# A two-model kernel on one Trainium2 core: three pieces of work are moved one unit of the weight stream later

## The chip, the cores and the metric

The kernel is one program on one core of one Trainium2 chip. The metric is the device time of one execution in microseconds, the median of several runs. Lower is better.

## What is computed

Two small models stand one behind the other, batch 1, 256 tokens, width 1024, all in float32. The first has two layers. Layer 0 mixes by gated linear attention, layer 1 by a recurrent mixer (mLSTM), and behind each mixer stands a mixture of 16 experts in which each token uses two:

```python
def mlstm_mixer(x, ...):                       # the recurrent mixer, 4 heads of 256
    qk, v, o_pre, gates = split(x @ w_in)
    q, k = split(silu(causal_conv(qk)))
    ... s = einsum('bhid,bhjd->bhij', q_n, k_n) * p
    num = ... + einsum('bhij,bhje->bhie', s, v_n);  den = ... + s.sum(-1)
    h = num / maximum(abs(den), exp(-m_row))
    return (head_norm(h) * sigmoid(o_pre)) @ w_out
def grouped_moe(t, ...):
    for e in range(16):
        h = silu(t @ w1[e]) * (t @ w3[e]);  y = y + gates[:, e:e + 1] * (h @ w2[e])
```

The second model has two layers of attention (8 query heads of one kind, 12 dilated ones in three groups) with rotary positions, a gate, and a feed-forward block of width 4096:

```python
    qa = axial_rope(rms(qa, q_norm_a[l]), row_cs, col_cs)      # rotation over rows and columns
    qb = apply_rope(rms(qb, q_norm_b[l, g]), *seq_cs)          # rotation over the sequence
```

## The kernel before, in words

**Weights and engines.** 420 MB of weights stream from HBM in chunks of 1 MB (128 x 2048 floats). SP issues every load in one fixed order and waits, chunk by chunk, until the buffer's last readers are done (`load`). A chunk is two *units* of 128 x 1024. Outside the experts a unit is split in two: ACT writes its rounded part `hi` (L1661), DVE the rest `lo` (L2111), and PE multiplies in three products. There are five `hi` and five `lo` buffers, so ACT may write unit n only when PE has used unit n-5. Experts' units are read unsplit.

**Order of the work.** There is one fixed list of steps per stage, written by a generator (`walk_gla`, `walk_moe`, `walk_mlstm`, `walk_attention`, `walk_ff`). Each engine runs through the same list and picks out its own part of each step, so moving a step moves it on PE, ACT and DVE alike. Waits are semaphores between the engines. Within an engine nothing overtakes.

**Side work.** `run_a` and `run_b` yield the matmuls of one projection, a job per unit, and behind each job call a function that advances a list of side steps (`Side.advance(n)` takes the next n of them). In the recurrent mixer the last projection before the output one is `og` (output gate, 8 jobs, numbered 0 to 7 here). Beside it run: the last head's scores (PE, then their weighting on DVE, L2104 `AR<-ps,AR`), four `values` steps on PE (each a few 128x1 products for the denominator, then 128x256 products), `den` (denominator, DVE from L2660), two `norm_stats` (L2275) and `norm_scale` (L2282 to the second L2104), `norm` 0 and 1 (ACT, L1705, four instructions each), `gated` 0 (DVE, L2104 `AR<-AR`, two instructions). An iterator `pace` says how many side steps follow each `og` job. Ahead of job 7 `gate_first` runs what is left, and PE turns (transposes) the gated rows, L991 (`turn` 0 and 1).

**Experts.** `walk_moe` first sorts tokens to experts. `gather` (g, k) is eight PE matmuls of 256 columns that collect rows for expert group g, columns 256k to 256k+255. Its result is written by ACT for even k in group 0 (L1821) and by DVE for odd k (L2101). Then come jobs `up` of 8 matmuls, four units each. The first one (job 0 here) reads gathers 0 and 1, the second (job 1) gathers 2 and 3.

**Attention.** The `qkv` projection has six segments of four jobs each. Behind a segment follow its rotation steps on DVE: sum, inverse root, norm, one `rope_turn` per rotation (segments 1 and 3 in `SEGS` have two, the others one) and `rope_add` (L2823). Then `qk_turn` on PE (L1491) turns its rows, and ACT copies them (L1987). `turns` holds how many jobs are still to pass before that, at first `LAG` = 2.

The longer of the two `pace` lists is:

```python
    pace = iter((0, 1, 2) + 13 * (3,))
    yield from run_b("og", 2, 8, feed, lambda: side.advance(next(pace)), end=gate_first)
```

Of the kernel before, what the change touches and what calls it, by code (L numbers as in the profile page):

```python
# [158 lines left out]
def run_a(name, mt, kt, feed, tick=None):  # L159
    for what, n, i in walk_a(mt, kt):  # L160
        if what == "unit":
            u, split = feed.unit()
            yield from split
        elif what == "mm":
            yield (name, n, i, u)
        elif what == "sink":
            yield (name + "_out", n)
        elif tick:
            yield from tick()
# [133 lines left out]
def walk_moe(feed, key):  # L303

    yield ("constants",)
    for g in range(4):
        yield ("ln_turn", g)
    yield ("router",)
    yield ("ln_stats",)
    yield ("logits",)  # L310
    yield ("sum_up", key)
    yield ("fill", 1)
    yield ("rows", 0, 0)
    yield ("affinity",)
    yield ("rows", 1, 0)
    yield ("x_hi", 0)
    for t in range(2):
        yield ("rows", t, 1)
    yield ("x_hi", 1)
    yield ("sum_row", key)  # L320
    yield ("ranks",)
    yield ("count",)
    yield ("x_lo", 0, 0)
    yield ("fill", 0)
    yield ("places",)
    yield ("one_hot", 0)
    yield ("x_lo", 1, 0)
    for t in range(2):
        yield ("x_lo", t, 1)
    for k in range(3):  # L330
        yield ("gather", 0, k)

    def beside(p, s):

        if s == 0:
            if p == 0:
                yield ("gather", 0, 3)
                yield ("sum_turn", key)
                for t in range(2):
                    yield ("ln_x", t, 0)  # L340
                    yield ("ln_x", t, 1)
                yield ("gates",)
                yield ("sum_out", key)
            if p in (0, 2, 4):
                yield ("one_hot", p // 2 + 1)
            if p == 1:
                yield ("turn", 0)
        if p > 1:
            for n in range(2):
                if s == (1 if p < 8 else 4):  # L350
                    yield ("scatter", p - 2, n)
        if p < 8 and s == (1 if p else 3):
            yield ("maps", p)
        if p == 7 and s == 1:
            yield ("overflow",)
        if p == 2 and s == 2:
            for n in range(2):
                yield ("carry", n)
        if 0 < p < 8 and s == 4:
            yield ("turn", p)  # L360
        if p < 6:
            for k, at in enumerate((1, 4) if p else (2, 3)):
                if s == at:
                    yield ("gather", p // 2 + 1, 2 * (p % 2) + k)

    for p in range(9):
        for s in range(6):
            if (p == 8 and s < 4) or (p == 0 and s > 3):
                continue
            us = []  # L370
            for _ in range(4):
                u, split = feed.unit()
                us.append(u)
                yield from split
            if s < 4:
                yield ("up", p, s // 2, s % 2, tuple(us))
            else:
                yield ("down", p - 1, s - 4, tuple(us))
            if s in (1, 3):
                yield (("silu", "gated")[s // 2], p)  # L380
            elif s > 3:
                yield ("y", p - 1, s - 4)
            yield from beside(p, s)
    for n in range(2):
        yield ("scatter", 7, n)
    yield ("open",)
    yield ("z_stats",)


def walk_mlstm(feed):  # L390
    def gates():
        yield []
        yield [("g_rows",)]
        yield [("g_cols",)]
        yield [("log_f", 0)]
        yield [("log_f", 1)]
        yield []
        yield [("f_cum",)]
        yield [("f_turn",)]
        yield [("run_max", 0)]  # L400
        yield [("run_max", 1)]
        yield [("run_max", 2)]
        yield []
        yield [("max_cols",), ("p_logits", 0)]
        yield [("p_logits", 1)]
        yield [("p_exp",)]
        yield [("p_mask",)]

    done = set()

    def scores():
        for h in range(4):
            while 2 * h + 1 not in done:
                yield []
            yield []
            yield [("scores", h)]

    def values():
        for hp in range(2):
            for t in range(2):  # L420
                yield [("values", t, hp)]
        yield [("den",)]
        yield [("norm_stats", 0)]
        yield [("norm_stats", 1)]
        yield [("norm_scale",)]
        yield [("norm", 0)]
        yield [("norm", 1), ("gated", 0)]

    side = Side(gates())
    yield from run_b("v", 2, 8, feed, side.advance)  # L430
    side.parts.append(scores())
    later = []
    for job in run_a("qk", 16, 8, feed, side.advance):
        if job[0] == "qk_out":
            done.add(job[1])
        if job[0] == "lo" and 6 in done:

            later.append(job)
            continue
        yield job  # L440
    yield from later
    side.parts.append(values())

    def gate_first():
        yield from side.drain()
        yield ("ln_gains",)
        yield ("turn", 0)
        yield ("turn", 1)

    pace = iter((0, 1, 2) + 13 * (3,))  # L450
    yield from run_b("og", 2, 8, feed, lambda: side.advance(next(pace)), end=gate_first)
    route = routing()
    rows = iter([[("ln_x", t, s)] for t in range(2) for s in range(2)] + 4 * [[]])
    yield from run_b("o", 2, 8, feed, lambda: route() + next(rows), half=lambda: (("turn", 2), ("turn", 3)), halved=True, staggered=True)


SEGS = [([(0, 8, 0)], []), ([(0, 2, 1), (128, 4, 2)], [(384, 2, 0)]), ([(0, 4, 3)], [(256, 4, 128)]),
        ([(0, 4, 4), (256, 4, 5)], []), ([(0, 4, 7)], [(256, 4, 384)]), ([(0, 4, 6)], [(256, 4, 640)])]
# [27 lines left out]
LAG, D1, D2 = 2, 3, 4  # L486
# [24 lines left out]
def walk_attention(feed, sums):  # L511
    turns, pending, pairs = [], [], []

    def rope(n):
        yield [("rope_sum", n)]
        yield [("rope_inv", n)]
        yield [("rope_norm", n)]
        for q in range(len(SEGS[n][0])):
            yield [("rope_turn", n, q)]
        turns.append([LAG, n])  # L520
        pending.append(n)
        yield [("rope_add", n)]

    def due():
        for x in list(turns):
            x[0] -= 1
            if x[0] < 0:
                turns.remove(x)
                pending.remove(x[1])
                yield ("qk_turn", x[1])  # L530

    def attention():
        while pending:
            yield []
        for j in range(PAIRS + D2):
            if j < PAIRS:
                due = [x for x in EXP_AT if EXP_AT[x] == j]
                yield [("score", j)] + [("exp", x) for x in due]
            if 0 <= j - D1 < PAIRS:
                yield [("probs", j - D1)]  # L540
            if j - D2 >= 0:
                i, n, of, *_ = SETS[2 * (j - D2)]
                if n == of - 1:
                    pairs.append(i)
                yield [("value", j - D2)]

    def with_turns(name, jobs):

        for job in jobs:
            if job[0] == name:  # L550
                yield from due()
            yield job

    side = Side()
    yield ("tables",)
    for job in with_turns("qkv", run_b("qkv", 6, 8, feed, lambda: side.advance(2))):
        yield job
        if job[0] == "qkv_out" and job[2] == 1:
            side.parts.append(rope(job[1]))
    side.parts.append(attention())  # L560
    yield from with_turns("gate", run_a("gate", 16, 8, feed, lambda: side.advance(2)))
    while len(pairs) < 2:
        yield from side.advance()
    yield from run_a("bb", 8, 2, feed, lambda: side.advance(2))
    yield from side.drain()
    side.parts.append(spread(0))
    yield from side.advance()
    yield from run_a("ba", 8, 4, feed, side.advance)
    yield from side.drain()
    yield from run_b("o", 2, 8, feed, halved=True, staggered=True, after=sums_up(sums))  # L570
# [2701 lines left out]
```

## Time and profile before

| | |
|---|---|
| Median of 3 runs | 1484.76 us (1483.83 to 1485.95) |
| Profiled execution, its own time | 1485.66 us |
| Profiled execution, span of the instructions | 1483.8 us |
| PE busy | 1443.6 us |
| DVE, ACT, POOL busy | 910.2, 626.7, 40.8 us |
| DMA | 420.17 MB, mean 283 GB/s |

The profiled execution's own time is 1.9 us longer than its span. Start and end of the program lie in that difference. Where the stages lie in the span: gated linear attention to 118 us, its experts to 332, recurrent mixer to 490, its experts to 711, then attention and feed-forward twice. A timeline row merges neighbouring instructions of one kind. In it the bracket gives the idle time of the engine just before and what ended it. A float32 product can leave two records on PE, so a count there can be twice the number of instructions.

### The profile page before, as it was taken

The numbers are of one execution on the slowest core, as the hardware profiler recorded it, in microseconds if no ns is written. First come the engines' busy times: TensorE is split into PE (matmuls) and PEld (weight loads), VectorE is DVE, ScalarE is ACT, GpSimd is POOL, SyncE is SP. The second block draws the span as 40 slices with busy tenths as digits, with TensorE's granted clock in tenths as the row PEclk, the third lists the DMA queues.
The fourth block names the chain that finished last, engine by engine and source line by source line (L and its number), as shares of the span: only waits on it lengthen the run. The fifth ranks groups of instructions, "written<-read, shape, count | busy, mean of one in ns | idle before, by whom it ended". The sixth has DMA issues, their size and how long they took to land.

```text
span 1483.8 us, 20474 instructions
## 1 busy us (share of the span) xinstructions
PE 1443.6 (97%) x8383; PEld 1068.5 (72%) x8383; DVE 910.2 (61%) x1549; ACT 626.7 (42%) x1004; POOL 40.8 (3%) x39
## 2 busy tenths in 40 slices
PE   9999999989999999999799999999999999999998
PEld 7885444436888544443578897999988898799997
DVE  4986111118787611111799888997968976775555
ACT  6453211115334321211555655454456566465443
POOL 0000000000000000000210000000002000000000
PEclk9999999999999999999899999999999999999999
DMA  9897999998467899999665463899955533445540
GB/s 379 314 365 301 426 427 426 427 426 329 166 247 297 331 424 427 427 426 426 247 231 184 181 232 142 335 369 352 357 182 187 197 123 125 151 170 193 179 168 29
DMA packets 59062, 420.17 MB, mean 283 GB/s; under 512 B 6657, under 2 KB 6721, under 8 KB 8658
## 3 DMA queue, kind: packets, MB, share of 16 engines
q1 hardware_dynamic: 58322, 417.17, 71.5%
q0 software_dynamic: 640, 1.61, 0.4%
q8 instruction: 69, 1.13, 0.3%
q14 instruction: 31, 0.25, 0.0%
HBM read 417.71 MB, written 1.05 MB: 282 GB/s over the span
## 4 chain that ended last, share of the span: by engine, by line
PE 80%; DVE 11%; DMA 4%; ACT 3%; issue 1%; SPq 0%; DVEq 0%; ACTq 0%
PE ps L869 78%; DVE lo L2111 2%; DMA AR<-in_moe 2%; DMA raw<-in_moe 2%; DVE AR L2104 2%; PE ps L1520 1%; DMA AR<-in_wgu 1%; DVE AR L2101 1%; PE ps L1491 1%; ACT AR L2011 1%; PE ps L1244 1%; DVE TINY L2104 1%; DVE ACC L2104 0%; PE ps L991 0%; PE ps L1001 0%
## 5 line engine op out<-in xcount | busy, mean ns | idle before, releaser
L2111 DVE TENSOR_TENSOR lo<-raw,hi 128x1024 fp32r<-128x1024 f32 x296 | 359.4, 1237 | 97.7 <-ACT hi L1661 97.0
L1661 ACT ACTIVATE hi<-raw 128x1024 fp32r<-128x1024 f32 x296 | 306.2, 1056 | 183.3 <-PE ps L869 178.1
L869 PE MATMUL ps<-T,hi 128*128 128x256 f32 x1792 | 323.8, 283 | 1.4 <-DVE lo L2111 0.6
L869 PE MATMUL ps<-hi,T 128*128 128x512 f32 x896 | 285.8, 396 | 1.0 <-DVE lo L2111 0.6
L869 PEld LDWEIGHTS ps<-T,hi 128*128 128x128 f32 x1792 | 277.1, 189 | 10.0 <-issue 5.1
L869 PE MATMUL ps<-T,lo 128*128 128x256 f32 x896 | 249.2, 280 | 0.0
L869 PEld LDWEIGHTS ps<-hi,T 128*128 128x128 f32 x896 | 169.0, 189 | 38.0 <-DVE lo L2111 2.1
L869 PE MATMUL ps<-lo,T 128*128 128x512 f32 x448 | 172.8, 390 | 0.0
L869 PEld LDWEIGHTS ps<-T,lo 128*128 128x128 f32 x896 | 169.2, 189 | 0.3 <-DVE lo L2111 0.3
L869 PE MATMUL ps<-hi,AF 128*128 128x512 f32 x512 | 163.3, 391 | 0.0
L2104 DVE SCALAR_TENSOR_TENSOR AR<-AR,ps 128x512 f32<-128x512 f32 x52 | 35.4, 684 | 192.0 <-PE ps L869 104.8
L869 PE MATMUL ps<-raw,TF 128*64 128x512 f32 x424 | 128.2, 595 | 3.0 <-issue 3.0
L869 PE MATMUL ps<-AR 128*64 128x512 f32 (+7 forms) x612 | 108.6, 408 | 4.7 <-POOL AR L2907 1.3
L869 PEld LDWEIGHTS ps<-hi,AF 128*128 128x128 f32 x512 | 96.2, 188 | 19.5
L869 PE MATMUL ps<-AR,TF 128*64 128x512 f32 x328 | 107.7, 595 | 0.5 <-DMA AR<-in_moe 0.5
L1857 ACT ACTIVATE AF<-ps,TINY 128x512 fp32r<-128x512 f32 x32 | 22.0, 688 | 195.5 <-PE ps L869 195.5
L2104 DVE SCALAR_TENSOR_TENSOR AF<-ps,TINY,AF 128x512 fp32r<-128x512 f32 x32 | 24.0, 750 | 124.6 <-ACT AF L1857 124.6
L869 PE MATMUL ps<-lo,AF 128*128 128x512 f32 x256 | 99.9, 390 | 0.0
L869 PEld LDWEIGHTS ps<-lo,T 128*128 128x128 f32 x448 | 84.5, 189 | 16.8
L869 PEld LDWEIGHTS ps<-raw,TF 128*64 128x64 f32 x424 | 39.5, 137 | 63.2 <-issue 62.4
L869 PEld LDWEIGHTS ps<-AR 128*64 128x64 f32 (+2 forms) x612 | 58.8, 163 | 33.6 <-issue 20.8
L2104 DVE SCALAR_TENSOR_TENSOR ACC<-raw,TINY,ACC 128x2048 f32<-128x2048 f32 x28 | 65.6, 2344 | 0.2
(247 smaller groups left out, 1730.5 us busy)
## 6 DMA issues: line engine op xcount, KB each, us to landing
raw<-in_moe SPq DMA_DIRECT2D x76, 1024.0 KB, 17.1
raw<-in_b_ff SPq DMA_DIRECT2D x64, 1024.0 KB, 5.3
AR<-in_moe SPq DMA_DIRECT2D x59, 1024.0 KB, 17.1
raw<-in_ada SPq DMA_DIRECT2D x48, 1024.0 KB, 6.7
ring<-in_moe SPq DMA_DIRECT2D x45, 1024.0 KB, 15.8
raw<-in_b_in SPq DMA_DIRECT2D x24, 1024.0 KB, 6.0
raw<-in_b_gate SPq DMA_DIRECT2D x16, 1024.0 KB, 4.8
ACC<-in_moe SPq DMA_DIRECT2D x12, 1024.0 KB, 20.2
```

The costliest lines, as they stand in the source:

```text
L869: return e.matmul(o, l, r, start=a, stop=z, skip_group_check=True)
L1244: ins = e.transpose(p[:, 128 * f:128 * f + 128], m.GR[:, 128 * f:128 * f + 128], ident)
L1491: ins = e.transpose(p[:, 256 * x + 128 * q:256 * x + 128 * q + 128], m.RT[n % 2][:, q, 128 * (p0 + x):128 * (p0 + x) + 128], ident)
L1520: ins = e.transpose(p[:, 256 * k + 128 * q:256 * k + 128 * q + 128], m.PB[j % 8][:, q, 128 * k:128 * k + 128], ident)
L1661: e.activation(hi[n % NC][:, :], raw[place[c]][:, 1024 * half:1024 * half + 1024], ACT.Copy).then_inc(*to("hi", "hi", n))
L1857: e.activation(m.YH[:, HALF[n]], PS[bank["down", i, x, n]][:, :], ACT.Copy, scale=m.GS[:, x:x + 1]).then_inc(*to("tile_out", "y_hi", i, x, n))
L2011: ins = e.activation(o, src, ACT.Exp, scale=m.SC, bias=mx[:, q:q + 1], accum_out=sm[:, 2 + 2 * k + q:3 + 2 * k + q])
L2101: return e.tensor_scalar(o, a, s1, s2, op0=op0, op1=op1)
L2104: return e.scalar_tensor_tensor(out=o, in0=a, scalar=s, in1=b, op0=op0, op1=op1)
L2111: tt(lo[n % NC][:, :], r, hi[n % NC][:, :], SUB).then_inc(*to("lo", "lo", n))
```

## The change

Three edits in the step lists, with no work added or removed.

1. Experts: `gather` (0, 2) is put behind job 0, next to `gather` (0, 3).
2. Recurrent mixer: `pace` is 0, 0, 1, 3, 3, ... in place of 0, 1, 2, 3, 3, ...
3. Attention: the turn of a segment with two rotations comes one job later (`LAG` + 1). The other segments stay.

```diff
@@ walk_moe
-    for k in range(3):
+    for k in range(2):
         yield ("gather", 0, k)
     def beside(p, s):
         if s == 0:
             if p == 0:
-                yield ("gather", 0, 3)
+                for k in (2, 3):
+                    yield ("gather", 0, k)
                 yield ("sum_turn", key)
@@ walk_mlstm
-    pace = iter((0, 1, 2) + 13 * (3,))
+    pace = iter((0, 0, 1) + 13 * (3,))
@@ walk_attention, rope(n)
-        turns.append([LAG, n])
+        turns.append([LAG + len(SEGS[n][0]) - 1, n])
```

Lines behind L337 have a number one higher in the changed kernel. POOL and SP keep their order in every row.

**DVE, recurrent mixer, from the last `conv` step to the denominator.** `AR<-ps,AR 128x384` weights the last head's scores, `ACC<-raw,TINY,ACC` is a step of the second model's modulation, the copy at the end opens `den`. Before:

```order
L2104 SCALAR_TENSOR_TENSOR AR<-AR 128x512
L2111 TENSOR_TENSOR lo<-raw,hi 128x1024 x3
L2104 SCALAR_TENSOR_TENSOR AR<-ps,AR 128x384
L2104 SCALAR_TENSOR_TENSOR ACC<-raw,TINY,ACC 128x2048
L2111 TENSOR_TENSOR lo<-raw,hi 128x1024 x2
L2660 COPY TINY<-ps 128x8
```

Now:

```order
L2105 SCALAR_TENSOR_TENSOR AR<-AR 128x512
L2112 TENSOR_TENSOR lo<-raw,hi 128x1024 x3
L2105 SCALAR_TENSOR_TENSOR ACC<-raw,TINY,ACC 128x2048
L2112 TENSOR_TENSOR lo<-raw,hi 128x1024
L2105 SCALAR_TENSOR_TENSOR AR<-ps,AR 128x384
L2112 TENSOR_TENSOR lo<-raw,hi 128x1024 x2
L2661 COPY TINY<-ps 128x8
```

The weighting now stands behind the modulation step and one more `lo`, and a further `lo` comes ahead of the denominator.

**ACT, recurrent mixer, around the norm.** `AR<-ps,TINY` are the eight norm instructions (four for each half of the heads), `T<-ps,TINY` follows the turn. Before:

```order
L1925 ACTIVATE AR<-ps 128x512 x2
L1661 ACTIVATE hi<-raw 128x1024 x2
L1705 ACTIVATE AR<-ps,TINY 128x256 x8
L1661 ACTIVATE hi<-raw 128x1024
L1714 ACTIVATE T<-ps,TINY 128x256 x4
```

Now:

```order
L1926 ACTIVATE AR<-ps 128x512 x2
L1662 ACTIVATE hi<-raw 128x1024 x2
L1706 ACTIVATE AR<-ps,TINY 128x256 x4
L1662 ACTIVATE hi<-raw 128x1024
L1706 ACTIVATE AR<-ps,TINY 128x256 x4
L1715 ACTIVATE T<-ps,TINY 128x256 x4
```

A `hi` part now stands between the two halves of the norm. On DVE its `lo` part stands ahead of the two `gated` instructions, behind which it stood before:

```order
L2296 TENSOR_TENSOR TINY<-TINY 128x8
L2105 SCALAR_TENSOR_TENSOR TINY<-TINY 128x8
L2112 TENSOR_TENSOR lo<-raw,hi 128x1024
L2105 SCALAR_TENSOR_TENSOR AR<-AR 128x512 x2
L2105 SCALAR_TENSOR_TENSOR T<-ps,TINY,T 128x256 x4
L2112 TENSOR_TENSOR lo<-raw,hi 128x1024
```

This is the changed order. Before, one `lo` stood behind `AR<-AR 128x512 x2` as well as the one ahead of it, and the `lo` ahead of it was of the unit before, which now stands between the two tokens' halves of `norm_stats`.

## Rows read from the trace of the kernel before

**Rows 1.** Page, part 1: busy us (share of the span) and instructions.
```profile
PE 1443.6 (97%) x8383; PEld 1068.5 (72%) x8383; DVE 910.2 (61%) x1549; ACT 626.7 (42%) x1004; POOL 40.8 (3%) x39
```

**Rows 2.** Timeline of PE, mixer's end: start, us, line, operation, count [idle before <-releaser].
```profile
440.69 1.55 PE L869 MATMUL ps<-AR 128*128 128x256 f32 x8 [1.29 <-DVE AR L2104]
442.00 0.47 PE L869 MATMUL ps<-hi,T 128*128 128x512 f32 x1
...
452.85 0.95 PE L869 MATMUL ps<-cst,AR 128*128 128x1 f32 x8
...
455.29 0.58 PE L869 MATMUL ps<-hi,T 128*128 128x512 f32 x1
...
463.46 0.39 PE L869 MATMUL ps<-hi,T 128*128 128x512 f32 x1
464.42 1.06 PE L991 MATMUL ps<-cst,AR 128*128 128x128 f32 x8 [0.57 <-DVE AR L2104]
...
468.51 0.47 PE L869 MATMUL ps<-hi,T 128*128 128x512 f32 x1 [0.25 <-DVE T L2104]
```

**Rows 3.** Timeline of DVE, the same stretch.
```profile
443.87 0.55 DVE L2104 SCALAR_TENSOR_TENSOR AR<-ps,AR 128x384 f32<-128x384 f32 x1
444.34 2.34 DVE L2104 SCALAR_TENSOR_TENSOR ACC<-raw,TINY,ACC 128x2048 f32<-128x2048 f32 x1
...
453.84 0.17 DVE L2660 COPY TINY<-ps 128x8 f32<-128x8 f32 x1 [4.89 <-PE ps L869]
...
461.41 0.17 DVE L2104 SCALAR_TENSOR_TENSOR TINY<-TINY 128x8 f32<-128x8 f32 x1
...
463.58 0.69 DVE L2104 SCALAR_TENSOR_TENSOR AR<-AR 128x512 f32<-128x512 f32 x1 [0.22 <-ACT AR L1705]
466.35 1.23 DVE L2111 TENSOR_TENSOR lo<-raw,hi 128x1024 fp32r<-128x1024 f32 x1 [2.08 <-ACT hi L1661]
```

**Rows 4.** Timeline of ACT, the same stretch.
```profile
461.61 3.76 ACT L1705 ACTIVATE AR<-ps,TINY 128x256 f32<-128x256 f32 x8 [2.10 <-DVE TINY L2104]
465.22 1.10 ACT L1661 ACTIVATE hi<-raw 128x1024 fp32r<-128x1024 f32 x1
```

**Rows 5.** Timeline of PE, start of attention layer 0.
```profile
756.89 1.97 PE L1491 MATMUL ps<-cst,AR 128*128 128x128 f32 x8 [2.65 <-DVE AR L2823]
```

**Rows 6.** Windows of 1 us: PE, PEld, DVE, ACT, POOL busy, PEclk, DMA share, GB/s.
```profile
729.00:730.00 1.00, 1.00 (x6) 0.87 (x5) 1.00 (x3) 0.91 (x2) 0.00 (x0) 0.95 0.00 0
759.00:760.00 1.00, 1.00 (x4) 0.77 (x3) 0.97 (x2) 0.49 (x1) 0.00 (x0) 0.59 0.64 156
```

**Rows 7.** Timeline of PE, ahead of attention, after its longest wait.
```profile
719.76 4.63 PE L869 MATMUL ps<-XLO 128*128 128x512 f32 x10 [6.65 <-DVE X L2104]
```

**Rows 8.** Timeline of ACT, then DVE, start of the first experts.
```profile
129.07 1.02 ACT L1821 ACTIVATE TF<-ps,vec 128x256 f32<-128x256 f32 x2 [1.18 <-PE ps L869]
...
130.01 1.00 DVE L2101 TENSOR_SCALAR TF<-ps,vec 128x256 f32<-128x256 f32 x2 [0.68 <-PE ps L869]
...
140.22 1.23 DVE L2207 TENSOR_TENSOR X<-X,AR 128x1024 f32<-128x1024 f32 x1
```

**Rows 9.** Timeline of SP's DMA issues, both experts' starts.
```profile
141.47 0.33 SPq L3005 DMA_DIRECT2D AR<-in_moe  x1
...
513.50 0.80 SPq L3005 DMA_DIRECT2D raw<-in_moe  x2
```

**Rows 10.** Windows of 4 us, both experts' starts, columns as in rows 6.
```profile
144.00:148.00 4.00, 4.00 (x24) 1.76 (x22) 0.24 (x1) 1.02 (x2) 0.00 (x0) 1.00 1.01 422
508.00:512.00 4.00, 4.00 (x24) 2.19 (x24) 2.48 (x4) 0.00 (x0) 0.00 (x0) 1.00 0.81 272
```

**Rows 11.** Waits of PE: line <- releaser: us in total, times, longest.
```profile
PE ps L1491 <- DVE AR L2823: 3.7, 2, 2.6
```

**Rows 12.** Timeline of PE, then DVE, second segment of attention layer 1.
```profile
1148.20 0.82 PE L1491 MATMUL ps<-cst,AR 128*128 128x128 f32 x6
...
1146.73 0.96 DVE L2823 TENSOR_TENSOR AR<-AR 128x768 f32<-128x768 f32 x1
```

## Prediction

> **What bounds the kernel now.** I read the page's busy times first: PE works 97% of the span [rows 1]. PE's work is the same before and after, so the edits can only change how long PE stands still. I then read the timelines of PE, DVE and ACT side by side at the places where steps move, looking for the bracket that shows a wait, and for the experts SP's issues and the DMA windows, since there the weights can be the bound.
>
> Three things are to be seen. In the recurrent mixer PE waits 1.29 us ahead of the last head's scores, 0.57 us ahead of the turn and 0.25 us ahead of the output projection [rows 2]. In the experts' stage the DMA engines are full from shortly after its start (share 1.01, 422 GB/s) [rows 10], so the stage ends when the stream ends, and the stream's last gap decides. In attention PE waits for a rotation twice in the whole program, 3.7 us together [rows 11].
>
> **Recurrent mixer, the scores.** The last scores follow `og` job 1 before and job 2 now. The 1.29 us wait goes: PE has job 2 (2.85 us) to run first. One job is (463.85 - 455.29) / 3 = 2.85 us, 463.85 being 463.46 + 0.39 [rows 2]. Without the wait job 1 ends at 440.69 - 1.29 = 439.40, job 2 at 442.25, the scores (442.00 - 440.69 = 1.31) at 443.56, job 3 at 446.41. Now the `values` steps stand there, and they need the weighted scores. DVE's weighting has moved behind the modulation step and one `lo`. DVE is free for the modulation step at 443.87 [rows 3]. That takes 2.3 and a `lo` 1.15 (rows 2.34 and 1.23, less the overlap with what follows of nearly 0.1), the weighting 0.55: ready at 447.87. PE starts 0.15 behind it, as at the turn (463.58 + 0.69 against 464.42), so at 448.0: **1.6 us of new wait**. Its bounds are 0, if DVE runs through faster than these rows, and 1.9. This is the first wait that takes the place of the one removed.
>
> **Recurrent mixer, the denominator.** Before, the last `values` step is behind job 3, and its denominator products end at 452.85 + 0.95 = 453.80 [rows 2]. DVE's copy starts at 453.84, after 4.89 us of standing idle [rows 3], so PE sets it. Now three `values` steps follow job 3 and the fourth job 4. The same point comes at 453.80 - 1.29 + 1.6 + 2.85 = 456.96, or 3.15 us later.
>
> **Recurrent mixer, from there to the turn.** DVE's chain of copy, statistics and scale has one `lo` in its middle before and now, and takes 453.84 to 461.58 [rows 3]. Before, ACT starts the norm at 461.61 (3.76 us for eight, so 1.88 for the first four), and the second `gated` instruction starts at 463.58. PE turns at 464.42, which is 2.84 us behind the scale [rows 2 to 4]. Now a `hi` stands between the norm's halves and its `lo` ahead of `gated`. Behind the scale come the four norms 1.9, `hi` until DVE starts its `lo` 1.13 (465.22 to 466.35), `lo` 1.15, two `gated` 1.3 (2 x 0.69 less the overlap), and 0.15 until PE starts: 5.63 us, **2.8 us longer**. The `hi` itself isn't late: it needs job 5, over by then. So the turn starts 3.15 + 2.8 = 5.95 us later, at 470.4. PE would get there at 463.85 - 1.29 + 1.6 = 464.2 and stands for 6.2 us where it stood for 0.57. The output projection's 0.25 us wait goes, as the turned rows then have job 7 as cover without DVE's `lo` in front.
>
> **TensorE's clock.** After a wait of 2.65 us PE starts again at 756.89 with the same kind of work, eight transposes and then 12-matmul jobs [rows 5], and the granted clock is at its lower level (1.2 GHz) until about 759.82 (mean 0.59 in that microsecond) [rows 6]. That is 2.9 us at half speed, a loss of 1.5. After the 6.65 us wait at 719.76, with a gap in the restart, the higher level returns only at about 729.1 [rows 6, 7]. For 6.2 us I take a loss of **1.5 us**, the nearer row in the work that follows. The ends are 0 and 4.0 (half of some 8 us of work in the second row). The Trainium skill, "TensorE: Matmul & The Clock Gate", section "Why this matters for your kernels", warns against exactly such gaps between bursts of matmuls, and its Part 1 says that one kernel had 6, 11 or 14 slow matmuls from run to run. At its 427 against 216 ns for 512 columns that is an estimate of 1.3 to 3.0 us, by which the sum would be up to 1.5 us higher.
>
> The mixer's part is 5.95 + 1.5 - 0.25 = **+7.2 us**. What waits for it further on moves with it: SP frees the experts' buffers in the mixer by the scores, the values, the gated rows and the norm, and behind them by PE's jobs.
>
> **Does the DMA stream swallow it?** In the second experts' stage the windows show a gap at the start (0.81 in 508 to 512) [rows 10]. SP can only issue the next loads once job 1 is done, 513.50 [rows 9]. A late PE makes this point late, and no load is ahead of it, so the delay passes 1:1.
>
> **Experts' third gather.** One gather is 0.94 us (ACT starts on gather 0 at 129.07, DVE on gather 1 at 130.01). Job 0 now follows gather 1 at once, but needs ACT's copy of gather 0, done at 129.07 + 1.02 = 130.09 [rows 8]. PE would come at 129.95 and starts at 130.15, **+0.2 us**. Job 0 frees two chunks some 0.7 us earlier, which is worth nothing if a later event rules the stream. In the first stage that event is the end of the normed rows X on DVE (140.22 + 1.23, SP issues at 141.47) [rows 8, 9], started by gather 3, which is 0.2 later. In the second it is job 1. So each stage costs 0.2, both **+0.4 us**. The bounds are -0.7 and +0.4 for each.
>
> **Attention's turns.** Of the twelve turns four move. The moved ones didn't wait: at 1148.20 there is no bracket, the sum was ready at 1147.69 [rows 12]. The two waits in the program are on the first segment's turn, with one rotation, which isn't moved. Nothing is to be gained and the transposes just stand between other jobs. Their readers (ACT's copy, the rotation two segments later, the scores) come later. I take 0, between 0 and +0.4 (0.1 for each).
>
> **Sum.** 7.2 + 0.4 + 0 = +7.6 us. On the profiled execution's own 1485.66 us this gives 1493.3. That execution is 0.9 above the median, and on the median the forecast is 1484.76 + 7.6 = **1492.4 us**. With the clock's loss at 0 or 4.0, the scores' wait at 0 or 1.9 and the gathers at their bounds, the case runs from 1487.7 to 1496, though all ends on one side are unlikely.
>
> **Rivals.**
> - *The mixer gains, as its 1.29 us wait goes and nothing is late.* The place is the turn ahead of job 7. It decides if `gated` is done before PE arrives at about 464. Then 1.29 + 0.57 + 0.25 go and 0.4 comes: 1483.1, no slower than before. For it speaks that DVE idles 4.89 us ahead of the copy; against it, that it idles because PE's products are late, which the change makes later. 7%. If the closed DMA gaps also count 0.7 each, it is near 1481.3; that needs both, 4% beside it.
> - *The stream swallows the delay.* If loads were queued beyond the slip when the second experts start, PE would catch up while it waits for weights: about 1485.2. The gap in 508 to 512 speaks against it. 6%.
> - *The clock returns late*, as after 719.76: 4.0 lost in place of 1.5, 1494.9. 12%, inside the range.
> - *Only the denominator's delay counts* (the new `hi` and `lo` cost nothing): 7.6 - 2.8 = 4.8, 1489.6. It decides if ACT starts that `hi` before the norm, which its order forbids. 8%, inside too.
>
> **How the numbers follow.** The forecast has 63%; with the last two rivals 83% lie at 1487.7 or more, so slower by over 0.2%. The range reaches from 1487.0, so that a partly swallowed delay is in it, to 1495.5. About 0.2% (3 us) is what a measurement of this kernel can tell from no change. Slower by more: 83%. Within it: 12%, the first and the second rival less one per cent. Faster by more: 5%, that one and the 4% beside the first rival.
>
> **What would show it.** In the changed profile PE should wait about 1.5 us ahead of the first 128x1 products, for DVE `AR` L2105, and about 6 us ahead of L992, followed by some 3 us of granted clock 0.5. The 1.29 us ahead of the scores should be gone, DVE's copy L2661 should start 3 us later, and ACT's norm should be split by a `hi`. The first job of each experts' stage should wait 0.2 us for ACT's `TF`. The attention rows should keep their distances. The forecast is wrong if PE's wait ahead of L992 is under 2 us, or if the second experts' stage ends less late than it begins.

## The result, and the profile after

The changed kernel takes **1497.62 us** (median of 4 runs, 1495.62 to 1499.07), against 1485.36 us (4 runs, 1483.83 to 1486.03) of the kernel before. The ratio is 1.0083, 95% interval 1.0066 to 1.0101: slower by 12.3 us, where 7.6 had been forecast. The sign and the places were right; the time lies 5.2 us above the forecast and 2.1 us above the range. Of the 5.2 us, 0.6 is that the kernel before has a median of 1485.36 with its fourth run and had 1484.76 with three.

The page of the changed kernel, parts 1 and 2 (busy time, then the span in 40 slices), answers to [rows 1]:

```profile
span 1496.3 us, 20472 instructions
...
PE 1447.8 (97%) x8383; PEld 1072.3 (72%) x8383; DVE 913.1 (61%) x1549; ACT 626.4 (42%) x1004; POOL 39.3 (3%) x39
...
PEclk9999999999998999999899999999999999999999
```

The number of PE's instructions is unchanged, yet PE is busy 4.2 us longer than the 1443.6 of before: the same work took more time. The slice of 449 to 486 us shows a clock of 8 tenths. (Lines of helpers behind L337 are one higher in the changed kernel, so L869 reads L870.) The timeline of PE in the mixer's end shows where that is (start us, us, line, operation, count [idle before <-releaser]); compare [rows 2]:

```profile
442.37 1.47 PE L870 MATMUL ps<-AR 128*128 128x256 f32 x8
...
446.22 0.39 PE L870 MATMUL ps<-hi,T 128*128 128x512 f32 x1
448.39 0.59 PE L870 MATMUL ps<-cst,AR 128*128 128x1 f32 x4 [1.78 <-DVE AR L2105]
448.84 2.06 PE L870 MATMUL ps<-AR 128*128 128x256 f32 x4
450.69 1.71 PE L870 MATMUL ps<-cst,AR 128*128 128x1 f32 x8
452.25 3.64 PE L870 MATMUL ps<-AR 128*128 128x256 f32 x8
...
456.09 1.11 PE L870 MATMUL ps<-AR 128*128 128x256 f32 x4
...
459.79 0.95 PE L870 MATMUL ps<-cst,AR 128*128 128x1 f32 x8
460.59 1.97 PE L870 MATMUL ps<-AR 128*128 128x256 f32 x8
...
474.03 1.94 PE L992 MATMUL ps<-cst,AR 128*128 128x128 f32 x8 [6.01 <-DVE AR L2105]
```

Two things are to be read here. First the waits: 1.78 us ahead of the values (forecast 1.6) and 6.01 us ahead of the turn (forecast 6.2); the 1.29 us ahead of the scores (442.37, no bracket) is gone. Then the durations: four products of 128x256 take 2.06 us at 448.84 and 1.11 us at 456.09, eight of 128x1 1.71 and 0.95, eight of 128x256 3.64 and 1.97. The same kind of work ran at nearly half speed, from 448.8 to about 455.6. The windows give the granted clock, the share of full speed behind the five busy times (columns as in rows 6):

```profile
448.00:450.00 2.00, 1.61 (x7) 1.47 (x8) 2.00 (x3) 0.18 (x1) 0.00 (x0) 0.70 1.04 434
450.00:452.00 2.00, 2.00 (x10) 1.82 (x9) 0.51 (x1) 0.00 (x0) 0.00 (x0) 0.50 1.00 422
...
454.00:456.00 2.00, 2.00 (x9) 1.61 (x8) 0.00 (x0) 0.00 (x0) 0.00 (x0) 0.59 1.00 422
456.00:458.00 2.00, 2.00 (x12) 1.73 (x12) 0.00 (x0) 0.00 (x0) 0.00 (x0) 1.00 1.03 434
...
472.00:474.00 2.00, 0.00 (x0) 0.00 (x0) 1.89 (x3) 1.25 (x3) 0.00 (x0) 0.68 0.00 0
474.00:476.00 2.00, 1.97 (x9) 2.00 (x10) 0.00 (x0) 0.84 (x2) 0.00 (x0) 0.50 0.00 0
...
478.00:480.00 2.00, 2.00 (x7) 1.59 (x6) 1.74 (x2) 0.60 (x1) 0.00 (x0) 0.62 0.00 0
```

The clock is at its lower level (0.50, which is 1.2 GHz) twice: behind the 1.78 us wait, until about 455.6, and behind the 6.01 us wait, until about 479.5. The first costs 3.3 us: from 448.39 to the last `values` step at 459.79 it is 11.40 us, and 8.08 for the same steps in the kernel with both waits filled (below). The second costs 2.6 us: from 474.03 PE's rows fall behind those of the kernel before by that much until the clock is back. The forecast had only the second, at 1.5.

VectorE's timeline of the same stretch, to be read against [rows 3]:

```profile
444.29 2.35 DVE L2105 SCALAR_TENSOR_TENSOR ACC<-raw,TINY,ACC 128x2048 f32<-128x2048 f32 x1
446.55 1.22 DVE L2112 TENSOR_TENSOR lo<-raw,hi 128x1024 fp32r<-128x1024 f32 x1
447.68 0.56 DVE L2105 SCALAR_TENSOR_TENSOR AR<-ps,AR 128x384 f32<-128x384 f32 x1
...
460.77 0.17 DVE L2661 COPY TINY<-ps 128x8 f32<-128x8 f32 x1 [10.26 <-PE ps L870]
...
468.35 0.17 DVE L2105 SCALAR_TENSOR_TENSOR TINY<-TINY 128x8 f32<-128x8 f32 x1
471.45 1.23 DVE L2112 TENSOR_TENSOR lo<-raw,hi 128x1024 fp32r<-128x1024 f32 x1 [2.94 <-ACT hi L1662]
472.60 1.29 DVE L2105 SCALAR_TENSOR_TENSOR AR<-AR 128x512 f32<-128x512 f32 x2
```

And ScalarE's, against [rows 4]:

```profile
468.55 1.93 ACT L1706 ACTIVATE AR<-ps,TINY 128x256 f32<-128x256 f32 x4 [7.51 <-DVE TINY L2105]
470.36 1.06 ACT L1662 ACTIVATE hi<-raw 128x1024 fp32r<-128x1024 f32 x1
471.30 1.94 ACT L1706 ACTIVATE AR<-ps,TINY 128x256 f32<-128x256 f32 x4
```

The weighting is done at 448.2, with the modulation step and a `lo` ahead of it, as forecast. The denominator's copy comes 460.77 - 453.84 = 6.93 us later than before: 0.4 from the experts upstream, about 3.15 from the order, the rest the clock. The norm is split by a `hi`, and the turn follows the start of the last scale by 474.03 - 468.35 = 5.68 us, where it was 464.42 - 461.41 = 3.01: 2.7 us more. By the turn the kernel is 474.03 - 464.42 = 9.61 us late, within 0.1 of 0.4 + 3.15 + 2.7 + 3.3. Behind the low clock it is 12.3 us late (PE turns the router's input `X` at 504.08 against 491.76), and it stays so: attention layer 0 starts its first turn at 769.66 against 756.89, 12.8 us late, and the end is 12.5 us late. The DMA stream in the second experts' stage took nothing back. The first job of that stage waits 0.27 us for ScalarE's `TF`, where 0.2 was forecast.

### The profile page after: what moved, and what is told of

Same layout as the page of the kernel before. It is cut to its first block, busy times and chain, and to the rows that moved or that the text cites. A ratio compares the mean times of both kernels' runs of the same rounds, so it can differ in the third digit from the quotient of the medians.

```text
span 1496.3 us, 20472 instructions
## 1 busy us (share of the span) xinstructions
PE 1447.8 (97%) x8383; PEld 1072.3 (72%) x8383; DVE 913.1 (61%) x1549; ACT 626.4 (42%) x1004; POOL 39.3 (3%) x39
## 4 chain that ended last, share of the span: by engine, by line
PE 79%; DVE 12%; DMA 4%; ACT 3%; issue 1%; SPq 0%; DVEq 0%; ACTq 0%
PE ps L870 77%; DVE lo L2112 3%; DMA AR<-in_moe 2%; DVE AR L2105 2%; DMA raw<-in_moe 2%; PE ps L1521 1%; DMA raw<-in_gla_qk 1%; DVE ACC L2105 1%; DVE AR L2102 1%; PE ps L1492 1%; ACT AR L2012 1%; PE ps L992 1%; PE ps L1245 1%; DVE TINY L2105 1%; DVE AR L2751 0%
## 5 line engine op out<-in xcount | busy, mean ns | idle before, releaser
L870 PE MATMUL ps<-T,hi 128*128 128x256 f32 x1792 | 323.8, 283 | 1.8 <-ACT hi L1662 0.8
L870 PE MATMUL ps<-hi,T 128*128 128x512 f32 x896 | 286.7, 397 | 0.9 <-DVE lo L2112 0.6
L870 PEld LDWEIGHTS ps<-T,hi 128*128 128x128 f32 x1792 | 277.4, 190 | 10.4 <-issue 5.1
L870 PE MATMUL ps<-T,lo 128*128 128x256 f32 x896 | 249.7, 281 | 0.0
L870 PEld LDWEIGHTS ps<-hi,T 128*128 128x128 f32 x896 | 169.8, 190 | 37.9 <-DVE lo L2112 2.0
L870 PE MATMUL ps<-lo,T 128*128 128x512 f32 x448 | 173.8, 392 | 0.0
L870 PEld LDWEIGHTS ps<-T,lo 128*128 128x128 f32 x896 | 169.5, 190 | 0.2 <-DVE lo L2112 0.2
L870 PE MATMUL ps<-hi,AF 128*128 128x512 f32 x512 | 163.5, 391 | 0.0
L870 PE MATMUL ps<-raw,TF 128*64 128x512 f32 x424 | 128.2, 595 | 3.1 <-issue 2.9
L870 PE MATMUL ps<-AR 128*64 128x512 f32 (+7 forms) x612 | 111.0, 413 | 3.4 <-POOL AR L2908 1.3
L870 PEld LDWEIGHTS ps<-hi,AF 128*128 128x128 f32 x512 | 96.3, 188 | 19.4
L870 PE MATMUL ps<-AR,TF 128*64 128x512 f32 x328 | 107.7, 595 | 0.7 <-DMA AR<-in_moe 0.4
L870 PE MATMUL ps<-lo,AF 128*128 128x512 f32 x256 | 100.1, 391 | 0.0
L870 PEld LDWEIGHTS ps<-lo,T 128*128 128x128 f32 x448 | 85.0, 190 | 16.9
L870 PEld LDWEIGHTS ps<-raw,TF 128*64 128x64 f32 x424 | 39.8, 137 | 63.2 <-issue 62.5
L870 PEld LDWEIGHTS ps<-AR 128*64 128x64 f32 (+2 forms) x612 | 60.4, 166 | 32.4 <-issue 20.9
```

Source lines behind the costliest of these rows:

```text
L870: return e.matmul(o, l, r, start=a, stop=z, skip_group_check=True)
```

## The experiments

All medians are set against the kernel before, run on the same chip between them: 1485.45 us (23 runs) for the first four kernels of the table, 1485.59 (27 runs, another chip) for the two that are caught up, for both waits filled and for "before, filled", 1485.04 (21 runs, a third chip) for the other three. The difference is that of the medians. The ratio is not worked out from these two medians, so the two columns can differ by some 0.1%, as for "before, filled".

| kernel | us | against before | ratio (95%) |
|---|---|---|---|
| mixer only | 1496.50 | +11.1 | 1.0072 (1.0060 to 1.0085) |
| gathers only | 1486.56 | +1.1 | 1.0007 (0.9998 to 1.0016) |
| turns only | 1485.43 | 0.0 | 0.9999 (0.9990 to 1.0007) |
| norm in one piece | 1491.01 | +5.6 | 1.0043 (1.0026 to 1.0060) |
| caught up | 1488.83 | +3.2 | 1.0021 (1.0010 to 1.0031) |
| caught up, wait filled | 1486.18 | +0.6 | 1.0002 (0.9993 to 1.0011) |
| mixer only, both waits filled | 1491.81 | +6.2 | 1.0046 (1.0032 to 1.0059) |
| mixer only, turn's wait filled | 1494.53 | +9.5 | 1.0062 (1.0048 to 1.0075) |
| norm in one piece, filled | 1488.05 | +3.0 | 1.0019 (1.0010 to 1.0028) |
| before, filled | 1484.54 | -1.1 | 1.0000 (0.9991 to 1.0009) |
| before, filled more | 1484.44 | -0.6 | 0.9995 (0.9986 to 1.0004) |

### One part of the change at a time

Mixer only:

```diff
-    pace = iter((0, 1, 2) + 13 * (3,))
+    pace = iter((0, 0, 1) + 13 * (3,))
```

> Only the mixer's side work is one unit later; the experts' gathers and the attention's turns stand as before. Theory A (the mixer alone carries the loss: denominator +3.15 us, the chain to the first turn +2.8 us, the clock at 1.2 GHz after a 1.8 us wait 3.3 us and after the 6.0 us wait 2.6 us, all passed on one for one): 11.9 us slower than before, 1497.2 to 1497.9 against 1485.6, with both stretches of low clock (near 448 to 455 us and near 473 to 479 us) in its windows. Theory B (the gathers or the turns contribute more than the trace of the whole change seems to say): less than 11 us slower. Theory C (the low clock near 448 us comes from the shift of the stage by the gathers, not from the wait): the first stretch is missing, and the kernel is about 8.6 us slower.

Gathers only:

```diff
-    for k in range(3):
+    for k in range(2):
         yield ("gather", 0, k)
...
-                yield ("gather", 0, 3)
+                for k in (2, 3):
+                    yield ("gather", 0, k)
```

> Only the third gather of both experts' stages stands behind job 0. By the trace of the whole change, each stage waits 0.27 us more for ScalarE at job 0 and the first one ends 0.41 us later: 0.4 us slower (0.3 to 0.6) expected, within 0.2% and so no difference that the rounds can tell from none. Rival: the gather one job later lets a write of the second stage's stream start earlier and gains up to 0.7 us a stage. Either way the part of the 12.5 us that is not the mixer's is under 1 us.

Turns only:

```diff
-        turns.append([LAG, n])
+        turns.append([LAG + len(SEGS[n][0]) - 1, n])
```

> Only the turns of the segments with two rotations are one unit later in both attention layers. By the trace of the whole change these turns come one job later (their times move by 2.5 to 2.9 us beyond the others) and nothing behind them moves: 0.0 us (-0.3 to +0.3). Rival: a score or a value product waits for a turned column and the end moves by up to 1 us; then a wait of PE on the turn's copies stands in its list of waits that before lacks.

Measured: +11.1, +1.1 and 0.0 us, together 12.2 where the whole change costs 12.3. The mixer carries the loss, the turns cost nothing that can be told from none (-1.5 to 1.0), and the gathers lie between -0.3 and 2.4 us: their expected 0.4 is in the interval, a gain beyond 0.3 is not. Both low stretches are in the mixer-only trace too (0.50 in the windows of 450 to 454 and of 474 to 478 us). So the gathers' shift is not what lets the clock fall, and theory C falls. The median is 0.8 us under the 11.9 worked out from one trace, which the interval (8.9 to 12.6) allows.

### The chain ahead of the turn

Against mixer only:

```diff
-    pace = iter((0, 0, 1) + 13 * (3,))
+    pace = iter((0, 0, 1, 3, 4) + 13 * (3,))
```

> As the mixer-only kernel, but from the fourth unit on the side work runs one unit further ahead: ScalarE does the eight norm operations in one piece with hi behind them, and VectorE does the gated products ahead of lo, as before the change. The denominator and the first wait on values stay late. Theory A (the order of norm halves, hi, gated and lo costs 2.8 us): 2.8 us less than the mixer-only kernel, so 9.1 us slower than before, and TensorE's wait ahead of the first turn falls from 6.0 to about 3.2 us; if its clock still falls after that shorter wait, the loss behind it stays near 2.6 us. Theory B (the wait ahead of the turn is set by the last scale of VectorE at 468.4 us alone, and the norm's order is covered): no difference to the mixer-only kernel. Theory C (a shorter wait keeps the clock up): 5.4 us less than the mixer-only kernel, 6.5 us slower than before.

Measured: +5.6 us (3.9 to 8.9), 5.5 less than mixer only. That is theory C's number; theory A's +9.1 lies just outside. The timeline of PE has the shorter wait:

```profile
470.34 1.06 PE L991 MATMUL ps<-cst,AR 128*128 128x128 f32 x8 [3.20 <-DVE AR L2104]
```

The wait fell from 6.0 to 3.2 us, so the order of norm, `hi`, `gated` and `lo` costs its 2.8. The clock held behind it in this execution: eight transposes take 1.06 us where they took 1.94. In the windows of this kernel the first low stretch is there, the second is not:

```profile
446.00:456.00 10.00, 8.52 (x33) 7.46 (x33) 3.61 (x4) 1.28 (x2) 0.00 (x0) 0.66 1.02 429
466.00:480.00 14.00, 10.52 (x50) 8.22 (x49) 10.37 (x21) 10.10 (x18) 0.00 (x0) 1.00 0.53 209
```

A wait of 3.20 us kept the clock, while one of 1.78 us in the same trace lost it. Its six runs spread from 1488.71 to 1495.46 us with mean clocks of 0.997 to 0.991, so in some of the others the clock may have fallen; only one was traced, and that the shorter wait keeps the clock is not shown.

### The first wait by itself, and filled

```diff
-    pace = iter((0, 1, 2) + 13 * (3,))
+    pace = iter((0, 0, 1, 5) + 13 * (3,))
```

> The mixer's side work is late in the second and third unit only and has caught up from the fourth on: the scores stand one job later and the first products of values in the fourth unit, the denominator, the norm and all behind them where they stood before the change. The wait of 1.3 us ahead of the scores goes and the one of 1.8 us ahead of the values comes. Theory A (TensorE's clock falls in that wait and the products behind it run at 1.2 GHz for some 6 us): 0.5 us from the waits and 3.3 us from the clock, 3.8 us slower than before, with a low clock near 448 to 455 us. Theory B (the low clock there needs the rest of the change too): 0.5 us slower, clock 1.00. In both, the wait ahead of the first turn stays near 0.6 us.

The same with the wait filled (in the step `values`, behind taking its bank of PSUM, the memory that matmuls write, and ahead of its waits; the sums of the seven products are overwritten):

```diff
                         p = take("values1", t, hp)
+                        if t == hp == 0:
+                            for _ in range(7):
+                                mm(p[:, :], T2[:, 1024:1152], T2[:, 0:512], True, True)
```

> As the caught-up kernel, with 7 products of 128x512 on a stale tile put into the wait ahead of the values; their sums are overwritten and nothing else changes. Theory A (the idle time lets the clock fall): TensorE has work in the wait, the clock stays at 1.00 from 448 to 456 us, and the kernel is 3.3 us faster than the caught-up one, 0.5 us slower than before (-0.3 to 1.0). Theory B (the short products of 128x1 behind the wait let it fall, wait or no wait): the clock still falls in 450 to 456 us and nothing is gained; then the products of values in the kernel before, at 1.00 without a wait, would need another reason.

Measured: +3.2 and +0.6 us. First the timeline of PE in the caught-up kernel, then in the filled one:

```profile
448.25 0.58 PE L869 MATMUL ps<-cst,AR 128*128 128x1 f32 x4 [1.77 <-DVE AR L2104]
448.69 1.27 PE L869 MATMUL ps<-AR 128*128 128x256 f32 x4
449.76 1.71 PE L869 MATMUL ps<-cst,AR 128*128 128x1 f32 x8
451.33 3.76 PE L869 MATMUL ps<-AR 128*128 128x256 f32 x8
```

```profile
446.80 1.75 PE L869 MATMUL ps<-T 128*128 128x512 f32 x7
448.64 0.61 PE L869 MATMUL ps<-cst,AR 128*128 128x1 f32 x4
449.11 1.11 PE L869 MATMUL ps<-AR 128*128 128x256 f32 x4
...
450.87 1.97 PE L869 MATMUL ps<-AR 128*128 128x256 f32 x8
```

The values start right behind VectorE's weighting in both (0.14 and 0.05 us behind its end); only what PE does in the 1.8 us ahead differs. With useless products there, the same eight products of 128x256 take 1.97 and not 3.76 us, and 2.6 us of the median come back. That shows the idle time as the cause and excludes theory B: the short products of 128x1 run at 1.00 when no idle time stands ahead of them. The +0.6 that is left (-1.0 to 1.6) agrees with the 0.5 us that the two waits were to be worth by themselves, but can't be told from none. One of the eleven runs of the caught-up kernel, untraced, took 1483.90 us at a mean clock of 0.998, the highest of the kernel before: in it the clock may not have fallen behind the wait at all, which no trace shows.

### Both waits filled

Mixer only, with the seven products above and 24 ahead of the first turn:

```diff
                 p = take("heads", i, g)
+                if i and not g:
+                    for _ in range(24):
+                        mm(p[:, :], T2[:, 1024:1152], T2[:, 0:512], True, True)
```

> As the mixer-only kernel, with 7 such products in the 1.8 us wait ahead of the values and 24 in the 6.0 us wait ahead of the first turn. The order and the waits of VectorE and ScalarE stay. Theory A (of the mixer's 11.9 us, 5.9 are the clock after these two waits): 6.0 us slower than before (5.5 to 7), 4.5 to 6 less than the mixer-only kernel, with 1.00 in all windows of 440 to 480 us. Theory B (the low clock is a companion of the loss and hardly carries it, since VectorE and ScalarE would be waited for anyway): within 1.5 us of the mixer-only kernel.

The 24 alone:

> As the mixer-only kernel, with 24 products in the 6.0 us wait ahead of the first turn alone; the wait ahead of the values stays empty. Theory A (the two losses of clock are apart and add): 2.6 us less than the mixer-only kernel, 3.3 more than the one with both filled: 9.3 to 9.5 us slower than before, low clock near 448 to 455 us, 1.00 from 470 to 480 us. Theory B (what the first loss costs is swallowed by the wait ahead of the turn): the same as the one with both filled, 6.2 us slower.

Measured: +6.2 (4.8 to 8.8) and +9.5 us (7.1 to 11.1), both near the number of theory A. PE's timeline of the first, from the values to the turn:

```profile
447.89 0.61 PE L869 MATMUL ps<-cst,AR 128*128 128x1 f32 x4
...
455.97 0.95 PE L869 MATMUL ps<-cst,AR 128*128 128x1 f32 x8
...
464.04 5.60 PE L869 MATMUL ps<-T 128*128 128x512 f32 x24
470.21 1.06 PE L991 MATMUL ps<-cst,AR 128*128 128x128 f32 x8 [0.57 <-DVE AR L2110]
```

and its windows, where both stretches now have the full clock:

```profile
446.00:456.00 10.00, 9.91 (x54) 8.36 (x53) 4.10 (x5) 1.55 (x2) 0.00 (x0) 1.00 1.01 424
466.00:480.00 14.00, 13.43 (x65) 10.94 (x64) 10.66 (x14) 9.47 (x17) 0.00 (x0) 1.00 0.35 130
```

The forecast of +5.95 for waits and order alone is what remains, within the interval. From 9.5 to 6.2 is the loss behind the first wait, 3.3 us. From 11.1 to 9.5 is the second's, 1.6 us against the 2.6 of the trace. The intervals reach some 1.9 us to either side, so by the medians both sizes stay rough. The traces are closer. PE's timeline of the kernel with the turn's wait alone filled:

```profile
449.94 0.58 PE L869 MATMUL ps<-cst,AR 128*128 128x1 f32 x4 [1.77 <-DVE AR L2107]
...
475.60 1.06 PE L991 MATMUL ps<-cst,AR 128*128 128x128 f32 x8 [0.57 <-DVE AR L2107]
```

From the first 128x1 products to the turn it is 25.66 us here, 25.64 in the changed kernel and 22.32 with both waits filled. So the 3.3 us lost behind the first wait arrive whole at the turn, whose wait swallows nothing of them, and filling the turn's own wait saves only what comes behind it: the two losses add.

### The denominator's delay alone

The norm in one piece, with the seven products and twelve ahead of the turn:

> As the kernel with the norm in one piece (fourth unit on one further ahead), with 7 products on a stale tile in the 1.8 us wait ahead of the values and 12 in the 3.2 us wait ahead of the first turn. What is left of the change in the mixer is the late denominator alone. Theory A (three terms that add: the denominator's delay 3.15 us, the order of norm, hi, gated and lo 2.8 us, the clock the rest): 3.2 us slower than before (2.7 to 3.7), and 3 us less than the kernel with both waits filled. Theory B (the order of the norm costs nothing of its own when the clock is kept): the same as the kernel with both waits filled, 6.2 us slower than before.

Measured: +3.0 us (1.5 to 4.2). Theory A: what is left is the denominator's 3.15, and against both waits filled (+6.2) the order of the norm is worth 3.2 us. The trace gives it without the noise of the medians:

```profile
448.48 0.61 PE L869 MATMUL ps<-cst,AR 128*128 128x1 f32 x4
...
467.99 1.06 PE L991 MATMUL ps<-cst,AR 128*128 128x128 f32 x8 [0.47 <-DVE AR L2110]
```

From the first products to the turn it is 19.51 us, against 22.32 with both waits filled: 2.8 us for the order of the norm.

### Can the kernel before be helped in the same way?

24 products ahead of its own 6.65 us wait, and 10 in each layer ahead of the first segment's turns (2.65 us in layer 0):

```diff
                         elif a[0] == 0 and l == 0:
+                            fill(XL1, ((24, 0, 0),))
                             fill(XL1, ((5, 0, 0), (5, 8, 8)), ("x", 3, 0, 1))
...
+                        if n == 0:
+                            f = PS[free[0]]
+                            if free[0] in freed:
+                                w.wait_ge(*after(*freed[free[0]]))
+                            for _ in range(10):
+                                mm(f[:, :], T2[:, 1024:1152], T2[:, 0:512], True, True)
                         w.wait_ge(*after("rope", l, n))
```

> The kernel before with such products in waits that it has anyway: 24 ahead of the first attention block's norm turns (the 6.65 us wait) and 10 in each layer ahead of the first segment's turns (2.65 us in layer 0, less in layer 1). Theory A (the clock that falls in these waits is paid for behind them): 1.5 us a layer at most behind the segment's turns, and 1.7 to 3 us behind the 6.65 us wait: 2 to 5 us faster than before, and the spread of its runs shrinks, since what varies from run to run is how long the low clock lasts. Rival (VectorE sets the pace behind these waits): no difference, within 0.5 us.

And with `fill(XL1, ((12, 0, 0),))` more behind the ten products:

> The kernel before with its own waits filled: 24 products in the 6.65 us wait ahead of the first norm turns, 12 more between the ten products that stand there and those turns, and 10 in each layer ahead of the first segment's turns. In the kernel with the first and the last of these alone, the low clock came all the same, after the wait ahead of the norm turns, which had grown from 1.3 to 3.3 us. Theory A (no wait left, no low clock left): clock 1.00 from 714 to 764 us, and 1 to 2.5 us faster than before. Rival (VectorE's norm sets the pace of that stretch): within 0.5 us of before.

Measured: 1.0000 (0.9991 to 1.0009) and 0.9995 (0.9986 to 1.0004), no difference to be told from none, and no version that beats both kernels. The 2 to 5 us expected of the first filling lie outside its interval. With the first filling the low clock only moved. The products that had run at half speed now end early, so the wait behind them grows, and the clock falls there (PE's timeline):

```profile
721.35 2.61 PE L869 MATMUL ps<-XLO 128*128 128x512 f32 x10 [1.19 <-DVE X L2111]
727.28 3.17 PE L1001 MATMUL ps<-cst,AR 128*128 128x128 f32 x16 [3.32 <-DVE AR L2108]
```

With the second it is gone altogether: the windows of that kernel, and those of the kernel before:

```profile
712.00:732.00 20.00, 18.07 (x83) 13.84 (x82) 16.93 (x45) 11.85 (x22) 2.38 (x3) 1.00 0.51 209
754.00:764.00 10.00, 9.59 (x48) 7.73 (x46) 9.73 (x21) 3.88 (x5) 0.00 (x0) 1.00 0.52 192
```

```profile
712.00:732.00 20.00, 12.05 (x43) 9.08 (x42) 17.66 (x46) 11.20 (x21) 2.38 (x3) 0.66 0.46 185
```

How much these stretches gave is read from PE's timeline of the kernel before and of the one filled more:

```profile
770.14 0.82 PE L1491 MATMUL ps<-cst,AR 128*128 128x128 f32 x6
```

```profile
758.04 1.09 PE L1499 MATMUL ps<-cst,AR 128*128 128x128 f32 x8 [0.41 <-DVE AR L2831]
...
769.90 0.82 PE L1499 MATMUL ps<-cst,AR 128*128 128x128 f32 x6
```

PE leaves the 6.65 us wait at 719.76 in the kernel before and at 721.27 in the filled one. From there to the first segment's turn (756.89 and 758.04) it is 37.13 and 36.77 us: a clock of 1.00 in place of 0.66 over 20 us brings only 0.4. DVE is busy for 17 of these 20 us, before and after, and the waits of both kernels there are for DVE. By these rows it is DVE that paces the norm, and a faster PE mostly waits longer. From the first segment's turn to the second's it is 13.25 and 11.86 us: there PE works without a wait, and the clock's fall behind the 2.65 us wait costs 1.4, as the prediction had read from [rows 5, 6]. Together that is 1.8 us between two traces. The medians don't confirm it (-0.6 us, interval -2.1 to 0.6). A reason that is not shown is that the kernel before may not lose it in every run. The low clock costs time, then, where PE is the engine that the others wait for. The rival holds for the norm, not for the turn behind it.

## Why the prediction was right or wrong

- **The scores' wait goes and one ahead of the values comes.** Right: 1.29 gone, 1.78 new for the 1.6 forecast, behind the same three DVE rows.
- **The denominator, +3.15.** Right: alone it measured +3.0 (1.5 to 4.2).
- **From there to the turn, +2.8.** Right: from the start of the last scale to the turn the trace has 5.68 us where 3.01 stood, 2.7 more; with the clock kept the traces give 22.32 - 19.51 = 2.8, the medians 6.2 - 3.0 = 3.2.
- **"TensorE's clock", 1.5 us.** This step failed, and it is nearly the whole miss. It priced the clock only behind the 6.2 us wait and let the new 1.6 us wait ahead of the values pass at full clock, for which it gives no reason. In the trace the clock cost 5.9 us, 3.3 behind the 1.78 us wait and 2.6 behind the 6.01; filling both gave some 4.8 us back on the median. Only the 1.29 us wait in [rows 2], with full-speed rows behind it, spoke for a harmless 1.6. The second size was also too small: of two rows, behind 2.65 and behind 6.65 us, it took the one with the shorter wait. 7.6 - 1.5 + 5.9 = 12.0, near the 12.3 measured. The sentence at the start, that with the same work the edits can only change how long PE stands still, is wrong for the same reason: PE's busy time grew by 4.2 us. The rival that let the clock return late had a loss of 4.0, again for one wait only.
- **The warning against gaps.** The Trainium skill, "TensorE: Matmul & The Clock Gate", section "Why this matters for your kernels", warns of idle gaps between bursts of matmuls, but only of gaps longer than the 1.78 us one. The trace agrees for the 6.01 us wait (2.6 us lost). It doesn't for the others: 1.78 us cost the most, 3.3, and behind 3.20 us, which that section would count as too long, the traced clock held. The measurement decides. The estimate worked out from the count of slow matmuls in Part 1 of the same page of the Trainium skill, 1.3 to 3.0 us for one fall, held the second loss and not the first; that count is of a kernel's start.
- **The delay passes 1:1.** Right: the kernel is 12.3 us late in front of the second experts, 12.8 us late at the start of attention, and 12.5 at the end.
- **Gathers +0.4, turns 0.** Right as far as can be told: +1.1 (interval -0.3 to 2.4) and 0.0 (-1.5 to 1.0).
- **The rivals.** That the mixer gains and that only the denominator counts are excluded by the 6.01 us wait and by the 2.8 us that the norm's order costs with the clock kept; that the stream swallows the delay, by the 12.8 us behind the second experts.
- **The bounds.** The low end of the prediction's case adds up to 1484.76 + 7.6 - 1.5 - 1.6 - 1.8 = 1487.5, and not to 1487.7; nothing hangs on it.

## What to carry to other kernels

Where TensorE paces a stretch, a new wait, even one of 1.8 us, can cost more than itself: add the half speed of what stands behind it to the range, once for every wait that a change makes or lengthens. Before a change is judged by its clock, fill the waits with useless matmuls of the same length; what comes back is the clock's share, what remains is the order's. Where another engine paces the stretch, the same filling gives little back (0.4 us here, in the norm), however low the clock stands in the page. And compare the distance between the same two rows in each kernel's trace: from the first 128x1 products to the turn it repeated within 0.1 us where order and clock were the same, when the interval of a median reached some 2 us to either side.

## What the runs showed of the hardware

- The length of a wait alone did not decide whether the clock fell. Behind 1.78 us ahead of the values it fell in every traced kernel that left that wait empty (five), while behind 3.20 us ahead of the turn it held in the one trace that has it. The clearest case is the first segment's turn of attention layer 0, the same work behind the same wait. The kernel before has 1.97 us for its eight transposes behind 2.65 us [rows 5]; the caught-up kernel (timeline of PE) has them at full clock, as have the kernel with the norm in one piece (1.09 us behind 2.66) and the one with the turn's wait filled (1.09 behind 2.65). In the changed kernel, mixer only, turns only and caught up with its wait filled they take 1.97 us behind 2.66 to 2.69:

```profile
760.93 1.09 PE L1491 MATMUL ps<-cst,AR 128*128 128x128 f32 x8 [2.63 <-DVE AR L2823]
```

What decides it there stays open: no experiment varies one wait's length, and each kernel has one trace.
- The fall came at no fixed distance behind the last work. In the changed kernel PE stopped at 446.6 and the clock fell near 448.8, after PE had started again; for the long wait it stopped at 468.0 and the clock fell near 472.7, while PE still stood. In the caught-up kernel the first four products of 128x256 behind the same wait still ran in 1.27 us, the next eight took 3.76.
- The same kernel has different clocks from run to run. The 27 runs of the kernel before beside the caught-up kernel had mean clocks of 0.992 to 0.998; the ten at 0.997 or more had a median of 1483.8 us, the four under 0.994 one of 1486.6. The clock is not all of the spread, though: the eleven runs of "before, filled more" were at 0.999 to 1.000 and still lay between 1483.10 and 1487.15. Part of it arises ahead of every edit: the last head's scores in the mixer start at 440.69 us in the trace of the kernel before and at 442.29 and 442.03 in the traces of the two "before, filled" kernels, which differ from it only further on.
